# A hybrid trunk step on one core: one adaLN block moved to the border of the layers, and the last tile's low parts made by TensorE and ScalarE

## The reference

```
mp = silu(cond) @ ada_w[l] + ada_b[l]            # shift, scale, gate, twice
h  = rmsnorm(x, norm_mix[l]) * (1 + scale) + shift
x += gate * mixer(h)      # layer 0: window attention | pooling; layer 1: 2-D Fourier per group
h  = rmsnorm(x, norm_ffn[l]) * (1 + scale) + shift
x += gate * moe(h)        # group of 4, then top 2 of 4 experts in it
```

## Time and profile before

| | |
|---|---|
| median of 3 runs | 771.26 us (770.49 to 771.87) |
| the profiled execution's own time | 771.06 us |
| its span, first to last instruction | 769.2 us |
| busy: TensorE, VectorE, ScalarE | 749.6, 393.5, 173.2 us |
| granted TensorE clock, mean | 0.996 |
| HBM read | 274.66 MB |

### The profile page before, as it was taken

One profiled execution on the slowest core, in us unless ns is written; L12 is line 12 of the kernel. 1 busy time (PEld: TensorE's weight loads), 2 busy tenths in 40 slices (PEclk: granted clock), 3 DMA queues, 4 the chain that ended last, 5 costly groups with the idle time before them and its releaser, 6 DMA issues.

```text
span 769.2 us, 9951 instructions
## 1 busy us (share of the span) xinstructions
PE 749.6 (97%) x3877; PEld 370.1 (48%) x3877; DVE 393.5 (51%) x844; ACT 173.2 (23%) x431; POOL 2.4 (0%) x12
## 2 busy tenths in 40 slices
PE   7999999998999999999998999998999999999997
PEld 3364546445544434534445658445545345444434
DVE  2216177947535336326337996636633454345326
ACT  4111574035310110110116103025311101110111
POOL 0000000000000000000000000000000000000000
PEclk9999999999999999999999999999999999999999
DMA  8979995268999999999999968056699999999994
GB/s 341 426 221 431 426 430 216 109 265 354 419 404 420 430 424 427 429 427 423 424 415 428 428 250 328 3 216 251 251 377 424 426 425 429 428 429 426 423 415 188
DMA packets 32850, 277.05 MB, mean 360 GB/s; under 512 B 7789, under 2 KB 8833, under 8 KB 12833
## 3 DMA queue, kind: packets, MB, share of 16 engines
q1 hardware_dynamic: 32305, 274.97, 86.5%
q10 hardware_dynamic: 432, 1.28, 0.5%
q0 software_dynamic: 64, 0.13, 0.0%
HBM read 274.66 MB, written 1.70 MB: 359 GB/s over the span
## 4 chain that ended last, share of the span: by engine, by line
PE 90%; DVE 3%; DMA 3%; ACT 2%; issue 1%; SPq 1%; DVEq 0%; ACTq 0%
PE bank L2146 29%; PE bank L2171 15%; PE bank L2011 11%; PE bank L2177 6%; PE bank L2125 6%; PE bank L2571 5%; PE bank L2445 4%; PE bank L1935 3%; DMA ring<-in_ada_w 3%; PE bank L2406 2%; PE bank L2157 1%; PE bank L2152 1%; PE bank L2497 1%; PE bank L2518 1%; PE bank L2100 1%
## 5 line engine op out<-in xcount | busy, mean ns | idle before, releaser
L2146 PE MATMUL bank<-ring,Z 128*64 128x512 f32 x1024 | 226.5, 594 | 0.0
L2146 PEld LDWEIGHTS bank<-ring,Z 128*64 128x64 f32 x1024 | 71.8, 137 | 137.6 <-issue 135.6
L2171 PE MATMUL bank<-ring,Z 128*64 128x512 f32 (+1 forms) x544 | 113.9, 570 | 0.0
L2011 PE MATMUL bank<-ring,T 128*128 128x512 f32 x192 | 83.6, 593 | 0.4 <-issue 0.4
L1620 DVE TENSOR_TENSOR Z<-Z,bank 128x512 f32<-128x512 f32 x16 | 11.0, 688 | 119.4 <-PE bank L2146 119.4
L2171 PEld LDWEIGHTS bank<-ring,Z 128*64 128x64 f32 x544 | 37.5, 137 | 68.3 <-issue 66.2
L1449 DVE SCALAR_TENSOR_TENSOR Z<-ring,cond,Z 128x512 f32<-128x512 f32 x84 | 59.3, 748 | 2.5
L2011 PEld LDWEIGHTS bank<-ring,T 128*128 128x128 f32 x192 | 36.0, 190 | 44.5 <-issue 44.5
L1614 DVE COPY Z<-bank 128x512 f32<-128x512 f32 x24 | 16.6, 692 | 73.2 <-PE bank L2125 73.2
L2177 PE MATMUL bank<-ys,Cs 128*128 128x512 f32 (+1 forms) x204 | 52.2, 391 | 1.1 <-DVE ys L1637 1.1
L1650 DVE TENSOR_TENSOR x<-x,bank 128x512 f32<-128x512 f32 x84 | 52.1, 682 | 0.3
(11 more groups left out here) (242 smaller groups left out, 738.1 us busy)
## 6 DMA issues: line engine op xcount, KB each, us to landing
ring<-in_moe_w SPq DMA_DIRECT2D x62, 2048.0 KB, 14.9
ring<-in_moe_w SPq DMA_DIRECT2D x60, 1024.0 KB, 10.3
ring<-in_ada_w SPq DMA_DIRECT2D x23, 2048.0 KB, 18.3
ring<-in_moe_w SPq DMA_DIRECT2D x16, 512.0 KB, 19.3
ring<-in_a_w_out SPq DMA_DIRECT2D x2, 2048.0 KB, 15.8
ring<-in_f_w_in SPq DMA_DIRECT2D x2, 2048.0 KB, 25.5
ring<-in_f_w_out SPq DMA_DIRECT2D x2, 2048.0 KB, 19.3
ring<-in_ada_w SPq DMA_DIRECT2D x2, 1024.0 KB, 7.8
```

Of the source, the lines that this page charges most:

```text
L2011: last = pe.matmul(b[:, :], T[:, k, i * P:(i + 1) * P], w[:, k, :], start=(k == 0), stop=(k == KT - 1))
L2146: last = pe.matmul(out[BLK * u:BLK * (u + 1), :], xT[:, b, k, s0 + BLK * u:s0 + BLK * (u + 1)], w[:, k, :], start=(k == 0), stop=(k == KT ...
L2171: last = pe.matmul(out, aT[:, k, BLK * u:BLK * (u + 1)], down_columns(w2, k, a, e), start=(k == 0), stop=(k == FC - 1), skip_group_check=True)
```

## The change

Two edits and what follows from them.

1. Block 20's product goes from the end of `route(0)` to the border, in front of that of 21. Its load goes from the end of `before0` to the head of `before1`; the positions behind it move by one. Block 21's product now uses bank 7 and waits for the last add into `x`. ScalarE and VectorE take their parts of block 20 at the border. In `route(1)` the three filler matmuls `busy(3)` are gone.
2. In both routers the low rows of the last tile no longer come from VectorE. `last_tokens` transposes into the bank with open accumulation, `low_tokens` adds the negated high part there (`minus_ident` times `h_high`), and ScalarE copies the result to `h_low` (`low_out`). The second matmul of it comes behind the next block's product. The gather waits for ScalarE in place of VectorE.

```diff
         t.empty(("logits", l))
-        t.fill(("tokens", l, 2, 0), "dve", bank=last_tile[0])
+        t.fill(("tokens", l, 2, 0), "act", bank=last_tile[0])
         for h in range(2):
             t.empty(("tokens", l, 1, h))
         t.add(("router", l), "dve", bank=others[0])
-        t.fill(("tokens", l, 2, 1), "dve", bank=last_tile[1])
+        t.fill(("tokens", l, 2, 1), "act", bank=last_tile[1])
         t.fill(("ada", n + 1), "dve", bank=others[1])
+        t.empty(("tokens", l, 2, 0))
         t.add(("gate", n, 0), "act", bank=others[0])
+        t.empty(("tokens", l, 2, 1))
         t.add(("rank", l), "dve", bank=first)
...
         t.add(("gate", n + 1, 1), "act", bank=others[1])
-        if l == 0:
-            t.fill(("ada", 20), "dve", bank=JOINED_BANK)
         of_gather[l] = [t.of[t.last[bank]][2:4] for bank in (2, 3)]
-        for h in range(2):
-            t.empty(("tokens", l, 2, h))
-        if l == 0:
-            t.empty(("ada", 20))
...
-    t.fill(("ada", 21), "dve")
+    t.fill(("ada", 20), "dve")
+    t.fill(("ada", 21), "dve", bank=7)
     norm(2, 0, 1, step=t.fill)
...
         t.empty(("norm", 2, 1, q))
-    t.empty(("ada", 21))
+    t.empty(("ada", 20))
     for q in range(2):
         t.empty(("norm", 2, 2, q))
+    t.empty(("ada", 21))
     early = [t.of[("norm", 2, i, q)][0] for i in range(2) for q in range(2)]
...
     before0 = ada_items[0:1] + w_in_items[0:1] + ada_items[1:4] + w_in_items[1:] + ada_items[4:13] + halves(a_w_out) + \
-        [ada_items[n] for n in (18, 19, 13, 20)]
+        [ada_items[n] for n in (18, 19, 13)]
     f_in, f_out = halves(f_w_in), halves(f_w_out)
-    before1 = [ada_items[21], f_in[0], ada_items[14], f_in[1], ada_items[15], ada_items[16], f_out[0], ada_items[17], f_out[1],
+    before1 = [ada_items[20], ada_items[21], f_in[0], ada_items[14], f_in[1], ada_items[15], ada_items[16], f_out[0], ada_items[17], f_out[1],
                ada_items[22], ada_items[23]]
...
     N_WOUT = [4 + 3 + 9, 4 + 3 + 10]
-    LATE = {n: N_WOUT[1] + 1 + i for i, n in enumerate((18, 19, 13, 20))}
-    N_FIN = [N_MIX1 + 1, N_MIX1 + 3]
-    N_FOUT = [N_MIX1 + 6, N_MIX1 + 8]
-    SECOND = {21: 0, 14: 2, 15: 4, 16: 5, 17: 7, 22: 9, 23: 10}
+    LATE = {n: N_WOUT[1] + 1 + i for i, n in enumerate((18, 19, 13))}
+    N_FIN = [N_MIX1 + 2, N_MIX1 + 4]
+    N_FOUT = [N_MIX1 + 7, N_MIX1 + 9]
+    SECOND = {20: 0, 21: 1, 14: 3, 15: 5, 16: 6, 17: 8, 22: 10, 23: 11}
...
         ssq, rsq = small[:, 96:126], small[:, 128:158]
+        minus_ident = sb_over("minus_ident", [P, P], F32R, "small")
         PC = sb("PC", [P, NH, P])
...
         h_high_out = sem("h_high_out")
+        low_full = sem("low_full")
         normed = sem("normed")
...
+            def gate_out(n, k):
+                l, cc = ADA[n]
+                s = 2 * l + (cc >= 10)
+                if k == 0 and s > 0:
+                    act.wait_ge(x_ready, NT * s)
+                b = stage_bank(("gate", n, k), act)
+                emptied_inc(act.activation(gate_b[:, k, HALF * (cc % 2):HALF * (cc % 2 + 1)], b[:, :], ACT.Copy))
             def ada_read(n):
-                l, cc = ADA[n]
-                if cc in GATE_CHUNKS:
-                    s = 2 * l + (cc >= 10)
-                    if s > 0:
-                        act.wait_ge(x_ready, NT * s)
+                if ADA[n][1] in GATE_CHUNKS:
                     for k in range(2):
-                        b = stage_bank(("gate", n, k), act)
-                        emptied_inc(act.activation(gate_b[:, k, HALF * (cc % 2):HALF * (cc % 2 + 1)], b[:, :], ACT.Copy))
+                        gate_out(n, k)
+            def low_out(l, hh):
+                b = stage_bank(("tokens", l, NT - 1, hh), act)
+                act.wait_ge(low_full, 2 * l + hh + 1)
+                cs = slice(HALF * hh, HALF * (hh + 1))
+                emptied_inc(act.activation(h_low[:, NT - 1, cs], b[:, :], ACT.Copy))
...
                     affine(2, 1)
+                    ada_product(20)
                     ada_product(21)
...
                 n = LAST_GATE[l]
+                low_out(l, 0)
                 ada_product(n + 1)
-                ada_read(n)
+                gate_out(n, 0)
+                low_out(l, 1)
+                gate_out(n, 1)
                 if l == 0:
                     ada_product(SUMMED[0][-1])
                 ada_read(n + 1)
-                if l == 0:
-                    ada_product(20)
                 moe(l)
...
                 dve.wait_ge(act_emptied, turn[("gate", MIX_GATE[l] + 1, 1)][3])
+                if l == 0:
+                    dve.tensor_scalar(minus_ident[:, :], ident, -1.0, None, ALU.mult)
                 for hh in range(2):
...
                 one_hot(pairs[l], QUAD)
-                low_part(l, NT - 1)
-                if l == 0:
-                    gate_parts(20)
                 dve.wait_ge(g_exp, l + 1)
...
             affine(2, 1)
+            gate_parts(20)
+            affine(2, 2)
             gate_parts(21)
-            affine(2, 2)
             def halves_apart(key, g, out, op0, op1):
...
+            def last_tokens(l, hh):
+                b = begin(("tokens", l, NT - 1, hh))
+                for q in range(4):
+                    last = pe.matmul(b[:, q * P:(q + 1) * P], T[:, 4 * hh + q, (NT - 1) * P:NT * P], ident,
+                                     start=(q == 0), stop=True, is_transpose=True, skip_group_check=True)
+                last.then_inc(full, 1)
+            def low_tokens(l, hh):
+                b = banks[turn[("tokens", l, NT - 1, hh)][0]]
+                pe.wait_ge(h_high_out, 2 * NT * l + 2 * (NT - 1) + hh + 1)
+                for a, e in high_pieces(NT - 1, hh):
+                    last = pe.matmul(b[:, a - HALF * hh:e - HALF * hh], minus_ident[:, :], high(NT - 1, a, e),
+                                     start=False, stop=True, skip_group_check=True)
+                last.then_inc(low_full, 1)
             def route(l):
...
                 last.then_inc(full, 1)
-                tokens_half(l, NT - 1, 0)
+                last_tokens(l, 0)
                 done_by(("logits", l))
...
                 last.then_inc(full, 1)
-                tokens_half(l, NT - 1, 1)
+                last_tokens(l, 1)
+                low_tokens(l, 0)
                 n = LAST_GATE[l]
                 ada_product(n + 1)
+                low_tokens(l, 1)
                 done_by(("ada", n))
...
                 ada_read(n + 1)
-                if l == 0:
-                    ada_product(20)
-                else:
-                    busy(3)
-            def busy(n):
-                for _ in range(n):
-                    pe.matmul(banks[7][:, 0:2 * P], ident, cst[:, 0:2 * P], start=True, stop=True)
...
                                     products(1, 0, early)
-                                pe.wait_ge(dve_emptied, turn[("tokens", l, NT - 1, 1)][3])
+                                pe.wait_ge(act_emptied, turn[("tokens", l, NT - 1, 1)][3])
                             last = products(0, t, part)
...
             moe(0)
+            ada_product(20)
+            pe.wait_ge(pairs[0]["back_out"], (NPAIR - 1) * 2 * NT + 3 * NT)
             ada_product(21)
```

## The result

The changed kernel took 772.97 us (median of 21 runs), the kernel before 771.09 beside it (21 runs). The ratio is 1.0026 [1.0019, 1.0033]: 1.9 us slower. The forecast was 770.1, range 768.7 to 772.0. The measured time lies above that range. The first profiled execution of the changed kernel was a disturbed one of 1975 us, so the rows here are of another execution of the same kernel, `after_again` (774.44 us, span 772.6).

> The changed kernel as it is, for a trace of a normal execution; the measured change is +2.0 us (+0.26%). Load theory: the first router gains about 2 us, and TensorE idles 3 us or more at the border for block 21 or the first half of f_w_in.

The account below looks back on a forecast made before the run. The prediction took TensorE to bound the kernel (90% of the chain), with loads as second limit. First router -2.1, border +1.1 and second router -0.2 gave -1.2 us: 771.26 to 770.1, range 768.7 to 772.0.

Parts of the forecast that it names:

- First router, -2.1 (1.7 to 2.4): Layer 0's router: without block 20's product the gather waits for `Sel`; first up product at 191.05 instead of 193.18.
- The delay of `Sel`: First router: `low_tokens` delays the rank matmul, so `Sel` comes 0.3 us later (0 to 0.5), at 188.5.
- The 0.35 us: First router: time of a 256-column VectorE operation; the negated identity's 128-column one is shorter and, being covered, costs nothing.
- Border, +0.9: Between the layers: block 20's product takes 2.1 us, less 1.25 of idle, so the norm's transposes start 0.9 later.
- Border, the loads, +0.2 (0 to 0.7): Between the layers: `f_w_in`'s first half lands at 418.4, wanted at 418.5, just in time; 0.2 us allowed.
- rival (c): Border: `f_w_in`'s first half lands late, at 421.3; 2.8 us of TensorE idle, +1.4 in all, 772.7; chance 0.09.
- The stream gains 2.1 + 0.6 = 2.7 us: Experts' loads of layer 0: slots come free 2.1 us earlier, SP within 0.6 of waiting; gain 2.7, not 4.9.
- Second router, -0.2 (-0.9 to +1.1): Layer 1's router: without filler the gather starts earlier, partly at half clock; up product 544.1, gain 0.5; -0.2 taken.
- rival (b): Second router: without filler the clock stays at 1.2 GHz, up product 1.1 us later; +0.1 in all, 771.4; chance 0.14.
- The rank matmul: Second router: it comes 0.5 us late, and VectorE, without slack there, is late by as much.
- The sum: Whole kernel: first router -2.1, border +1.1, second router -0.2 make -1.2 us; forecast 770.1, chance 0.45.

Follow-up runs that it names:

- after_busy: The changed kernel with the three filler matmuls of the second router put back behind the gate reads; 772.34 us, 1.0017 against the kernel before.
- split_keep: Changed kernel with fillers ahead of the second router's gate reads and warm-up cut into 16 pieces instead of 6, same columns; 771.72 us, 1.0014 against the kernel before.
- after_pad2: The changed kernel with 2 tiny products (4 matmuls in the trace) added to the warm-up at the start; 774.38 us, 1.0040 against the kernel before.
- after_keep: The changed kernel with filler matmuls ahead of the second router's gate reads, none ahead of the gather; 771.19 us, 1.0003 against the kernel before.
- after_pad11: The changed kernel with 11 tiny products (22 matmuls in the trace) added to the warm-up at the start; 776.71 us, 1.0052 against the kernel before.
- move: The kernel before with block 20 alone moved; low rows stay with VectorE and the filler stays; 771.56 us, 1.0007 against the kernel before.

## Why the prediction was wrong

- **First router, -2.1 (1.7 to 2.4).** Right: -2.26. The gather waited 0.27 us for ScalarE's gate copy, the copies of the low parts were hidden, the first up product came 3.54 us after the gather began. The delay of `Sel` was smaller than forecast: VectorE read the ranks 4.45 us behind the router product in place of 4.36, 0.1 us for 0.3. (The 0.35 us that the prediction puts down to the earlier trace rows stands in no row there; the trace of the kernel before has it at 187.33, L1489.)
- **The experts of layer 0, no term.** This is the step that failed. The sum let TensorE's gain pass through 219.6 us of experts untouched, and looked for its enemies among the loads at the far end. 2.0 of the 2.26 us were lost in the last pair, to the fetch of TensorE's own code, whose position the change had moved. No row of the kernel before shows a wait there; the transfers on the queue of instructions and the branch ahead of the last pair are what could have raised the question.
- **Border, +0.9.** Right in kind, too large: +0.62, as the product costs 1.96 and not 2.1 us, and the transposes came 4.92 us after the last back product in place of 4.30.
- **Border, the loads, +0.2 (0 to 0.7), and rival (c).** In the changed kernel's profiled execution the load cost nothing, with the 2 us of the stall to its help; in `after_busy`, the same program up to there, it cost 1.14 us all the same. Without the stall it is 1.14 us (`split_keep`) and more. "The stream gains 2.1 + 0.6 = 2.7 us" was too much: with block 20's load gone from behind the router, nothing else could be issued, and from 180 to 210 us the transfers ran at 339 GB/s in place of 376. That is 1.1 MB, or 2.6 us of the 4.9 that the absent block leaves. Landing in `split_keep` was 420.0 with a first router 0.8 us later than before, so 419.2 on the time scale of the kernel before, where I had 418.4 for a want at 418.5; the want was 418.1. So (c) was the right rival at a smaller size, 1.1 in place of 2.8 us, and would have taken half of what the first router gains. (Its landing of 421.3 doesn't agree with the 421.1 that the border's own sum gives.)
- **Second router, -0.2 (-0.9 to +1.1), and rival (b).** The rank matmul came 0.47 us later as forecast (4.14 us behind the router product in place of 3.67). The clock was the wrong choice between two ends that I had, and the second term that was off: (b) said +1.1, the profiled execution shows +1.4. In `after_pad2` the same code had one half-clock stretch in place of two and took 12.68, so executions differ by this. Between the ratios of the changed kernel and `after_keep` lie 1.8 us; with the clock kept by fillers the stage gives -0.95, and not -0.2.
- **The sum.** -2.26 + 2.0 + 0.6 + 0.1 and, for the second router, between 0 and +1.4: 0.5 to 1.9 us. The measured +1.9 is the upper end; a late `f_w_in` (1.1) and the loads of layer 1's last pair (0.9) come on top in some executions, and the kernel before has its own two groups, so the median can't be split more finely from one trace each. The forecast had -1.2. With the missing term alone it would have been +0.8; with (b) as well it is +2.1.

## What to carry to other kernels

Before a change that adds or removes instructions on the busiest engine far ahead of a jump, look where its code transfers lie in time; a gain in one stage counts only once the stages behind it are seen to keep their length. Fill an engine's idle time where it is idle, ahead of the instruction that it waits to issue: three fillers behind the gate reads ran at half clock and held the gather back, the same three ahead of them showed no cost and the clock stayed for the gather (12.70 and 11.49 us). And a load that is taken out of the front of a full stream gives back only what the stream can issue in its place: compare GB/s in that stretch before counting it.

## What the runs showed of the hardware

- TensorE stood still for 0.7 to 2.3 us (0.9 to 3.0 us of stage) in the middle of a product with its data there, 1, 5 or 8 matmuls behind the branch ahead of the last pair, where the program ahead of it was 17, 21 or 24 matmuls shorter than in the kernel before. From 1 shorter to 3 longer it did not stand still; nothing between was run. The profile calls it "issue", and the transfer on the instruction queue starts 2.4 to 2.5 us before it ends. Why the fetch begins only behind the pair's first matmul, and not when the branch is reached, these runs don't show.
- Matmuls of 16 columns, one behind the other at the start of `after_pad11`, took 0.11 us each: 22 took 2.52 us at a granted clock of 1.00. Each has a weight load of its own, and these start 0.11 us apart as well.
- A stretch with TensorE busy 1.45 of 3.41 us (`move`) was followed by one of granted clock 0.50, and so was one with 1.16 of 3.41 (changed kernel); the Trainium skill (TensorE: Matmul & The Clock Gate, Part 1) has activity release the clock, and filling the idle time did so here: 3.56 of 4.54 us busy, clock 1.00 behind it.
